# Rebuilding the second layer's dilated attention: products per token, norm factors in the weights, one maximum over the three groups, V held beside ones

## The chip, the cores and the metric

The kernel runs on one core of one Trainium2 chip. The metric is the device time of one execution in microseconds (us), the median of several runs. An instruction runs on TensorE (PE, its weight loads are PEld), VectorE (DVE), ScalarE (ACT) or GpSimd (POOL); SyncE (SP) issues most of the transfers.

## The reference, cut to what matters

One inference step of a two-layer decoder trunk on 512 new prompt tokens and 8 decode tokens (520 rows of 1024, float32). Layer 0 is stick-breaking attention and a mixture of experts. Layer 1, which the change touches, is attention over three dilated windows, and a second mixture of experts:

```python
kv = (rmsnorm(x, g_kv) @ w_kv).reshape(b, t, N_DIL, 2, N_KV_B, HEAD_DIM)     # 3 groups, 4 K/V heads of 64
k = rope(rmsnorm(kv[:, :, :, 0], k_norm), pos)                               # v = kv[:, :, :, 1]
q = rope(rmsnorm(rmsnorm(x, g_attn) @ w_q, q_norm), pos)                     # 3 groups, 16 query heads of 64
# group g attends over a window with dilation 1, 4, 16: o[g], lse[g]
# (the first over the block before and its own, the others here within the tokens of one residue)
w = softmax(stack(lses), axis=0)                                             # over the three groups
x = x + einsum('gbth,gbthe->bthe', w, stack(outs)).reshape(...) @ w_o
```

The normed and rotated K, and V, are outputs too. `rmsnorm(x, g)` is `x * rsqrt(mean(x*x) + eps) * g`.

## The kernel before

The stages follow one another, each in a block that ends with all engines meeting: layer 0's attention, its mixture of experts (`moe`), `layer_b`, then `moe` again. `moe` leaves two weighted rows per token in DRAM (`y_rows`). Its last block (L1347 to L1395) reads them back and adds them to the residual `x` (L1391), token tile by token tile; for layer 0 ACT squares each tile (L203) and POOL forms the factor `rs` (L211, L212).

`layer_b` (L1398) works on units: a unit is one K/V head j (0 to 3) in one group g, with 64 columns of V, 64 of K and 4 x 64 of the query heads that share them, 384 in all (`UW`), for all 520 tokens. `WINDOW` sets the order of groups in a head: 1, 2, 0. First `turn_normed` (L221) multiplies `x` by `rs` and by each of two gain rows (L252), turns the results so that the 1024 channels lie on partitions (L264) and copies them out (L242): `xkT` and `xqT`. The unit weights are fetched while this goes on (`load_unit`, L1416, queued by SP), and after that whenever a unit's products are done.

In the attention block PE follows an order written out by hand (`weave`, L1570):

- `project` (L1528): 128 of the 384 columns are the stationary operand, 260 tokens move. Six such chunks of 8 products each make a unit, and their results have tokens along the row: ACT copies them (L1689) and PE turns them back to tokens on partitions (`turn_tok`, L1547, L1555 and L1560), DVE copies these to `tok` (L1781).
- POOL then norms and rotates K and Q of the unit (`front`, L1899 to L1925). Only after this are K and Q turned again (`turn_back`, L1578), 12 transposes of 128x128 in a unit, and copied by ACT (L1709). The kernel runs two units ahead: the parts of `project` and `turn_tok` for unit n+2 are woven between the steps of unit n (`ahead`).
- For each of the 4 query heads in turn: `qk` (L1585), the scores in PSUM, four products of 64 rows x 128 columns (group 0: two of 128 and three of 256); `soft` on DVE (L1806 scales and masks, L1809 takes the maximum of each row, L1810 negates it); `exps` on ACT (L1715), which also sums; `turn_p` (L1604), `p_copy` on ACT (L1723), `pv` (L1613) with the turned probabilities as the stationary operand and V moving, 64 columns, and `o_copy` on DVE (L1814).
- Groups 1 and 2 have their tokens ordered by residue (t mod 4), so their outputs go to DRAM and back (`reorder`, L1492) to be put in order.
- `combine` on DVE (L1832) weighs the three groups by their maxima and sums; `turn_o` on PE (L1664) turns the result, DVE copies it to `oT` (L1869).

One pass of this loop over j takes three units. The next block has the output projection (L317, L326) and the decode tokens' attention.

Of the kernel before, what the change touches and what calls it, by code (L numbers as in the profile page):

```python
# [43 lines left out]
for _name, _width in (("ident", 128), ("tri", 128), ("strict", 128), ("ones", 128),  # L44
                      ("cos", NT * 8), ("sin", NT * 8), ("valid", NT), ("iota", NE), ("iota99", NE),
                      ("iota64", CAP), ("gid", 2 * NT), ("sid", 2 * NT), ("m0", 4 * 256), ("m1", 128), ("m2", 128), ("m3", 128), ("pidx", 1), ("sel8", DEC), ("eps", 1), ("eps64", NT), ("mhalf", NT)):
    CONST[_name] = (_at, _at + _width)
    _at += _width
# [4 lines left out]
def constants():  # L53
# [19 lines left out]
    put("sin", np.sin(ang))  # L73
    put("valid", np.stack([np.arange(128) < rows for _, rows in TILES], 1))
# [51 lines left out]
def flat(ap):  # L126
    return ap.rearrange("p a b -> p (a b)")

def build(nc, a, outs):  # L130
# [5 lines left out]
    o_rows = [nc.dram_tensor(f"o_rows{g}", [SEQ, 4 * 66], F32, kind="Internal").ap() for g in range(2)]  # L136
# [3 lines left out]
    with ExitStack() as ctx:  # L140
# [38 lines left out]
        ss, rs = sb("ss", [128, NT]), sb("rs", [128, NT])  # L179

# [633 lines left out]
        def moe(layer, norm, next_norm):  # L814
# [6 lines left out]
            wts = sb("wts" + L, [128, 2, NT], to=phM)  # L821
# [523 lines left out]
            last_norm[0] = norm  # L1345

            with ExitStack() as ph, nc.Block() as block:  # L1347
                yr = sb("yr" + L, [128, 2 * NT, D], to=ph)
                s_gt, s_cb = [lsem(f"y_back{k}") for k in range(2 * NT)], lsem("y_added")
                junk = sb("junk_c" + L, [128, D], to=ph)  # L1350
# [6 lines left out]
                @block.sync  # L1357
                def _(sp):
                    rows_back(sp, 0)
                    if next_norm:  # L1360
                        next_norm.load(sp)
                    else:
                        for t, rows in TILES:
                            sp.wait_ge(s_cb, 2 * t + 2)
                            dst = y_prompt[0, 128 * t:128 * t + 128, :] if t < 4 else y_sample[:, 0, :]
                            sp.dma_start(dst, x[0:rows, t, :]).then_inc(s_out, 16)
                        sp.wait_ge(s_out, 16 * NT)

                @block.scalar
                def _(act):  # L1370
                    rows_back(act, 1)
                    if next_norm:
                        for t in range(NT):
                            act.wait_ge(s_cb, 2 * t + 2)
                            next_norm.square(act, t, junk)

                @block.gpsimd
                def _(pool):
                    if next_norm:
                        pool_do.on(pool)  # L1380
                        for t in range(NT):
                            next_norm.power(pool, t)
                        pool_do.done()
# [14 lines left out]
        def layer_b(norm, next_norm):  # L1398

            phX = ExitStack()  # L1400
            UW = HD + KQ
            wB = sb("wB", [128, NDIL, KT, UW], to=phB)
            xkT = sb("xkT_b", [128, KT, TOK], to=phX)
            xqT = sb("xqT_b", [128, KT, TOK], to=phX)
# [4 lines left out]
            WINDOW = (1, 2, 0)  # L1409
            s_w = [sem(f"wb{g}_in") for g in range(NDIL)]  # L1410

            def kv_cols(j, g, part):

                return ds(g * 512 + part * 256 + j * HD, HD)

            def load_unit(sp, j, g):  # L1416
                sp.dma_start(wB[:, g, :, 0:HD], w_kv[:, :, kv_cols(j, g, 1)]).then_inc(s_w[g], 16)
                sp.dma_start(wB[:, g, :, HD:2 * HD], w_kv[:, :, kv_cols(j, g, 0)]).then_inc(s_w[g], 16)
                sp.dma_start(wB[:, g, :, 2 * HD:], w_q[:, :, ds(g * D + j * 256, 256)]).then_inc(s_w[g], 16)

            def first_units(sp):
                for g in WINDOW:
                    load_unit(sp, 0, g)

            norm.turn([xkT, xqT], prefetch=first_units)

# [3 lines left out]
            with phX, ExitStack() as ph, nc.Block() as block:  # L1430
                pT = sb("pT", [128, 3, TOK], to=ph)
                tok = sb("tok", [128, NDIL, NT, UW], to=ph)
                kk = sb("kk", [128, 4, 2 * HD], to=ph)
                kT = sb("kT", [128, SEQ], to=ph)
                qT = sb("qT", [128, 2, SEQ], to=ph)
                vp = sb("vp", [128, 2, 4, HD], to=ph)
                sc = sb("sc", [128, 2, 4, 256], to=ph)
                pTs = sb("pTs", [128, 2, 8 * 128], to=ph)
                nm = sb("nm", [128, 2, 4], to=ph)
                junk = sb("junk_b", [128, 1], to=ph)  # L1440
                ost = sb("ost", [128, NDIL, 4, 4, HD + 2], to=ph)
                cw = sb("cw", [128, 5, 4, 4], to=ph)
                ce = sb("ce", [128, NDIL, 4, 4], to=ph)
                oc = sb("oc", [128, 4, 4, HD], to=ph)
                ot = gain_row[:, :].rearrange("p (t h e) -> p t h e", t=4, h=4)
# [4 lines left out]
                s_kvo = [sem(f"b_kv_stored{g}") for g in range(NDIL)]  # L1450
                (s_gn, s_gain, s_proj, s_pev, s_tt, s_tk, s_vc, s_rope, s_tb, s_tbc, s_qk, s_sev, s_mx, s_ex, s_tp,
                 s_ptc, s_pv, s_oc, s_od, s_ob, s_cm, s_ce, s_comb, s_to, s_toc, s_kk) = (
                    sem("b_" + n) for n in (
# [655 lines left out]
```

## Time and profile before

| | us |
|---|---|
| median of 3 runs (1758.04 to 1768.62) | 1766.94 |
| the profiled execution, its own time | 1769.61 |
| its span, first to last instruction | 1767.8 |
| y rows asked for by SP, end of layer 0's experts | 747.07 |
| first projection of `layer_b` | 785.60 |
| last instruction of its attention block ends | 1337.08 |

### The profile page before, as it was taken

The page shows a single profiled execution, that of the slowest core. Times are in us where ns is not written, and L with a number is a line of the kernel's source. Part 1 is how long each engine was busy: PE and PEld are TensorE (multiplying, and loading weights), DVE is VectorE, ACT ScalarE, POOL GpSimd, SP SyncE. Part 2 cuts the span into 40 slices and gives each one's busy share as a digit, 9 for nine tenths or more (in the row PEclk, how much of TensorE's full clock was granted, in tenths as well). Part 3 has the DMA queues.
Part 4 walks back from the last instruction along what each step waited for, and adds up shares of the span by engine and source line. Part 5 has one row for each costly group of instructions (what it writes and reads, how often), then busy time and mean ns, then how long its engine had stood idle before and what let it go on. Part 6 is the DMA issues. An engine that isn't in the chain of part 4 may idle for free. (4 is left out here: it accounts for less than half of the span.)

```text
span 1767.8 us, 21720 instructions
## 1 busy us (share of the span) xinstructions
PE 1478.4 (84%) x8250; PEld 1069.6 (61%) x8250; DVE 606.3 (34%) x917; ACT 448.8 (25%) x959; POOL 485.3 (27%) x522
## 2 busy tenths in 40 slices
PE   5899999697699988559998998998885986999882
PEld 4677777443666554347887877887772444666451
DVE  1354443311411111161335436346335723111113
ACT  2233443311122211131333332433430111222110
POOL 3343334300011110015664564455400000111100
PEclk9999999899599999869999999999756966999997
DMA  7834323400989999462221221210305237999994
GB/s 265 290 103 135 104 72 108 168 1 0 350 318 421 420 421 420 201 206 58 75 75 43 67 63 42 66 33 0 126 27 154 94 119 300 412 420 421 421 409 169
DMA packets 148834, 335.72 MB, mean 190 GB/s; under 512 B 51832, under 2 KB 101464, under 8 KB 124064
## 3 DMA queue, kind: packets, MB, share of 16 engines
q1 hardware_dynamic: 133760, 296.73, 45.0%
q0 software_dynamic: 13824, 33.84, 5.3%
q10 hardware_dynamic: 1184, 4.26, 0.6%
q8 instruction: 43, 0.70, 0.2%
q14 instruction: 23, 0.19, 0.0%
HBM read 312.74 MB, written 38.55 MB: 199 GB/s over the span
## 5 line engine op out<-in xcount | busy, mean ns | idle before, releaser
L917 PE MATMUL ps<-wg,oT 128*64 128x256 f32 x1024 | 237.1, 385 | 19.3 <-DMA wd<-in_w_down 17.8
L917 PE MATMUL ps<-wu,oT 128*64 128x256 f32 x1024 | 237.3, 386 | 0.0
L917 PEld LDWEIGHTS ps<-wg,oT 128*64 128x64 f32 x1024 | 139.7, 139 | 75.7 <-DMA wd<-in_w_down 28.2
L1543 PE MATMUL ps<-xqT_b,wB 128*128 128x260 f32 x768 | 185.0, 397 | 0.0
L455 PE MATMUL ps<-xnT_a,wA 128*128 128x260 f32 (+1 forms) x768 | 172.7, 385 | 2.5 <-DMA wA<-in_w_qkv_a 1.3
L1543 PEld LDWEIGHTS ps<-xqT_b,wB 128*128 128x128 f32 x768 | 148.4, 197 | 24.2 <-issue 1.0
L455 PEld LDWEIGHTS ps<-xnT_a,wA 128*128 128x128 f32 x768 | 145.8, 192 | 27.0 <-issue 4.1
L917 PEld LDWEIGHTS ps<-wu,oT 128*64 128x64 f32 x1024 | 139.6, 139 | 36.3 <-issue 16.4
L1308 POOL DMA_INDIRECT y_rows<-ysb,idx x32 | 32.1, 1002 | 435.5 <-DVE ysb L952 435.5
L935 PE MATMUL ps<-wd,hT 128*64 128x512 f32 x512 | 124.0, 601 | 30.4 <-DVE hT L946 30.4
L778 POOL TENSOR_TENSOR work<-work,cst 128x128 f32<-128x128 f32 x128 | 74.5, 582 | 184.8 <-DVE work L703 147.5
L1806 DVE SCALAR_TENSOR_TENSOR sc<-ps,cst 128x512 f32<-128x512 f32 (+1 forms) x48 | 41.6, 867 | 194.5 <-PE ps L1600 112.5
L943 DVE TENSOR_TENSOR h<-sg,ps 64x256 f32<-64x256 f32 x64 | 26.4, 413 | 237.5 <-ACT sg L940 231.1
L1715 ACT ACTIVATE sc<-sc,nm 128x128 f32<-128x128 f32 (+1 forms) x192 | 81.3, 425 | 77.6 <-DVE nm L1810 77.6
L1905 POOL TENSOR_TENSOR sq<-tok 128x1600 f32<-128x1600 f32 x12 | 34.2, 2852 | 230.2 <-DVE tok L1781 230.2
L1543 PE MATMUL ps<-xkT_b,wB 128*128 128x260 f32 x384 | 94.6, 404 | 1.1 <-PEq L156 1.0
L508 PE MATMUL ps<-work,cst 128*128 128x128 f32 (+3 forms) x288 | 68.2, 399 | 31.0 <-POOL work L790 31.0
L952 DVE COPY ysb<-ps 64x512 f32<-64x512 f32 x64 | 44.4, 694 | 137.1 <-PE ps L935 137.1
L317 PE MATMUL ps<-wB,oT 128*128 128x512 f32 (+1 forms) x160 | 77.5, 649 | 12.0 <-DVE x L326 10.1
L1543 PEld LDWEIGHTS ps<-xkT_b,wB 128*128 128x128 f32 x384 | 75.9, 202 | 13.3 <-issue 1.3
L508 PEld LDWEIGHTS ps<-work,cst 128*128 128x128 f32 x288 | 49.3, 215 | 51.3 <-POOL work L790 34.3
L935 PEld LDWEIGHTS ps<-wd,hT 128*64 128x64 f32 x512 | 36.6, 136 | 70.2 <-issue 70.2
(263 smaller groups left out, 2336.6 us busy)
## 6 DMA issues: line engine op xcount, KB each, us to landing
wg<-in_w_gate SPq DMA_DIRECT2D x64, 1024.0 KB
wu<-in_w_up SPq DMA_DIRECT2D x64, 1024.0 KB
wd<-in_w_down SPq DMA_DIRECT2D x64, 1024.0 KB
wA<-in_w_qkv_a SPq DMA_DIRECT2D x24, 512.0 KB, 4.3
wB<-in_w_q_b SPq DMA_DIRECT2D x12, 1024.0 KB
wB<-in_w_kv_b SPq DMA_DIRECT2D x24, 256.0 KB
o_rows<-ost SPq DMA_DIRECT2D x8, 528.0 KB, 5.3
ost<-o_rows SPq DMA_DIRECT2D x8, 528.0 KB
```

The costliest lines, as they stand in the source:

```text
L317: last = nc.tensor.matmul(bank(6 + n)[0:rows, :], oT[:, m, 128 * t:128 * t + rows], self.w[m][:, 512 * n:512 * n + 512], start=(m == 0), s ...
L455: last = nc.tensor.matmul(bank(6 + h)[:, 0:half], wA[:, m, k, :], xnT[:, k, half * h:half * h + half], start=(k == 0), stop=(k == KT - 1))
L508: return nc.tensor.matmul(ps[:, b + o:b + o + width], lhs, rhs, start=start, stop=stop, skip_group_check=True)
L778: last = nc.gpsimd.tensor_tensor(v, v, mask, op)
L917: last = nc.tensor.matmul(bank(q)[lo:lo + CAP, 0:FE], x[:, k, :], wt[:, k, :], start=(k == 0), stop=(k == KT - 1))
L935: last = nc.tensor.matmul(bank(4 + q)[CAP * n:CAP * n + CAP, :], hT[:, q, f, :], wd[s][:, f, 512 * n:512 * n + 512], start=(f == 0), stop= ...
L952: return nc.vector.tensor_copy(ysb[w][CAP * q:CAP * q + CAP, 512:D], bank(4 + q)[CAP:2 * CAP, :])
L1308: pool.indirect_dma_start(out=y_rows, out_offset=rows_of(idx, 1, v), in_=ysb[v % 2][:, :], in_offset=None, bounds_check=2 * TOK - 1, oob_i ...
L1543: last = nc.tensor.matmul(bank(h)[:, 0:HALF], wB[:, g, kt, 128 * f:128 * f + 128], xT[:, kt, HALF * h:HALF * h + HALF], start=(kt == 0), s ...
L1715: last = nc.scalar.activation(sc[:, h % 2, b, 0:width], sc[:, h % 2, b, 0:width], ACT.Exp, bias=nm[:, h % 2, b:b + 1], accum_out=ost[:, g, ...
L1806: V.scalar_tensor_tensor(out=dst, in0=src, scalar=SCALE, in1=mask, op0=ALU.mult, op1=ALU.add).then_inc(s_sev, 1)
L1905: pool_do(P.tensor_tensor(sq[:, :, :], kq, kq, ALU.mult))
```

## The change

Only `layer_b` and what leads into it change; `moe` for layer 1 is as before.

- The adding of the experts' rows moves into the attention block. `x` is turned as it is, unnormed (`turn_x`), and there is one turned copy, `xT`.
- The gains `g_kv` and `g_attn` lie on partitions (`gcol`), and DVE multiplies each unit's weights by them, in place, before its first product (`scale`, two instructions, 8x128 and 8x256 elements a partition). The factor `rs` of a token is applied when its products are copied from PSUM. Groups 1 and 2 use it in residue order (`rsr`, which goes through DRAM once).
- `project`: 128 tokens of `xT` are the stationary operand, 384 weight columns move; for groups 1 and 2 the tokens are picked by residue, with tables `cosr`, `sinr` for the rotation. Four chunks of 8 products, one chunk of 8 products for the last 32 tokens in four column groups (32 columns wide each), and one product with `sel8` that sums these four. DVE copies each chunk from PSUM (`evict`) straight to `tok` and to `vo`, which holds V (64 columns) beside ones (64 columns). The ACT copies of projections, `turn_tok`, the turned V copy, the doubling copy into `kk` (now into `tok`) and their waits are gone. Three units are projected ahead instead of two, and the groups come in the order 0, 1, 2.
- Scores come in 8 steps in a pass (4, 2, 2) rather than 12, each for two heads, whose products alternate between partitions 0 to 63 and 64 to 127 and between two banks; `soft` takes 1024 elements in each step and keeps all scores of the pass in SBUF.
- One maximum per token and head: `far_max` and `near_max` join the groups' maxima; since they are in two orders, they cross through DRAM (`m_rows`, 16-byte pieces). The exponentials (`exps`, without a sum) start only after it, so after all scores of the pass.
- The probabilities are turned in 8 parts (`PARTS`; far = groups 1 and 2 of a head, near = group 0), half of each copied by ACT and half by DVE (`p_copy`). `weigh`: `vo` is the stationary operand and the turned probabilities move, 128 columns. The output is turned already, with its sum in partitions 64 to 127. `finish_head` on DVE copies the far half in token order, adds the near half, takes the reciprocal of 64x512 sums and multiplies into `oT`. `combine`, `turn_o`, `reorder` and `o_copy` go.

The diff, cut to what the prediction speaks of:

```diff
+                    def turn_x(t, rows):
+                        pe.wait_ge(s_cb, 2 * t + 2)
...
+                            for kt in range(KT):
+                                last = nc.tensor.matmul(bank(c % 2)[:, 0:UW], xT[:, kt, cols], wB[:, g, kt, :],
+                                                        start=(kt == 0), stop=(kt == KT - 1))
...
+                    def scores(j, g, s):
...
+                            return nc.tensor.matmul(bank(4 + h)[:, o:o + width], qT[r, pair, 128 * b:128 * b + 128],
+                                                    kT[r, 128 * kb:128 * kb + width], start=True, stop=True)
...
+                        if g:
+                            for b in range(4):
+                                for h in range(2):
+                                    last = product(h, b, b, 128 * b, 128)
...
+                                for g in (1, 2):
+                                    o = 512 * (g - 1) + 128 * b
+                                    last = nc.tensor.matmul(out, vo[:, j % 2, g, b, :], P[:, o:o + 128],
+                                                            start=(g == 1), stop=(g == 2))
...
+                        turn_back(j, 0, 0)
+                        turn_back(j, 0, 1)
+                        ahead(0, 0)
+                        turn_back(j, 0, 2)
+                        ahead(0, 1)
+                        scores(j, 0, 0)
+                        ahead(0, 2)
+                        scores(j, 0, 1)
+                        ahead(0, 3)
+                        scores(j, 0, 2)
+                        ahead(0, 4)
+                        scores(j, 0, 3)
+                        ahead(0, 5)
...
+                        turn_back(j, 2, 0)
+                        turn_back(j, 2, 1)
+                        ahead(1, 4)
+                        turn_back(j, 2, 2)
+                        ahead(1, 5)
+                        scores(j, 2, 0)
+                        ahead(2, 0)
+                        scores(j, 2, 1)
+                        ahead(2, 1)
+
+                        turn_p(j, 0)
+                        ahead(2, 2)
+                        turn_p(j, 1)
+                        weigh(j, 0)
+                        ahead(2, 3)
...
+                        turn_p(j, 3)
+                        weigh(j, 2)
+                        ahead(2, 5)
+                        for i in range(4, NPART):
+                            turn_p(j, i)
+                            weigh(j, i - 1)
+                        weigh(j, NPART - 1)
...
+                    def scale(j, g):
+                        dve.wait_ge(s_w[g], 48 * j + 48)
+                        for i, (lo, hi) in enumerate(((0, 2 * HD), (2 * HD, UW))):
+                            w = wB[:, g, :, lo:hi]
+                            V.tensor_tensor(w, w, gcol[:, i].unsqueeze(2).to_broadcast([128, KT, hi - lo]), ALU.mult).then_inc(s_ws, 1)
...
+                            V.tensor_scalar(tok[:, g, c, HD:], bank(c % 2)[:, HD:UW], r, None, ALU.mult)
+                            V.tensor_scalar(vo[:, j % 2, g, c, 0:HD], bank(c % 2)[:, 0:HD], r, None, ALU.mult).then_inc(s_ev, 1)
+                        elif c == 4:
+                            V.tensor_copy(part[:, :], bank(0)[:, 0:UW]).then_inc(s_ev, 1)
...
+                    def finish_head(j, h):
+                        dve.wait_ge(s_pv, NPART * j + PARTS.index((h, 1)) + 1)
+                        b = 2 + 2 * (h % 2)
+                        dve_do(V.tensor_copy(osum.rearrange("p (i r) -> p r i", r=4), bank(b).rearrange("p (r i) -> p r i", r=4)))
+                        V.tensor_tensor(osum, osum, bank(b + 1), ALU.add).then_inc(s_oc, 1)
+                        dve.wait_ge(s_oc, 4 * j + h + 1)
+                        dve_do(V.reciprocal(orec[0:HD, :], osum[HD:2 * HD, :]))
+                        dve_do(V.tensor_tensor(oT[64 * (h % 2):64 * (h % 2) + 64, 2 * j + h // 2, 0:SEQ], osum[0:HD, :], orec[0:HD, :], ALU.mult))
...
+                        soft(j, 0, 2)
+                        if more:
+                            scale(j + 1, 1)
+                        ahead(0, 4)
+                        soft(j, 0, 3, s_m0)
+                        ahead(0, 5)
...
+                        ahead(1, 3)
+                        if more:
+                            scale(j + 1, 2)
+                        ahead(1, 4)
+                        ahead(1, 5)
...
+                        p_copy(j, 3)
+                        finish_head(j, 0)
+                        ahead(2, 5)
+                        p_copy(j, 4)
+                        finish_head(j, 1)
+                        if j < NKV - 2:
+                            scale(j + 2, 0)
+                        p_copy(j, 5)
+                        p_copy(j, 6)
+                        finish_head(j, 2)
+                        p_copy(j, 7)
+                        finish_head(j, 3)
```

In the last part, which is DVE's, `ahead` is `evict` of the next pass's unit. Before its product c, `project` waits for the eviction of product c-2 of the same bank, and product 5 for that of product 4. `turn_p(i)` waits for the exponentials of part i and both copies of part i-1, `weigh(i)` for both copies of part i.

## Rows read from the trace of the kernel before

**Rows 1.** Table by stage: window, length, busy PE PEld DVE ACT POOL, clock, DMA share, GB/s
```profile
747.00:785.60 38.60, 13.34 (x80) 11.97 (x81) 25.36 (x20) 14.39 (x20) 8.03 (x10) 0.62 0.81 248
...
1104.30:1230.60 126.30, 119.02 (x678) 101.05 (x677) 56.85 (x86) 43.50 (x139) 66.56 (x52) 0.96 0.12 35
1230.60:1337.10 106.50, 82.23 (x379) 70.44 (x376) 45.30 (x74) 35.95 (x121) 28.05 (x24) 0.63 0.17 64
```

**Rows 2.** Timeline of PE in a pass: start, us, line, operands, records, [idle before]
```profile
1154.13 1.16 PE L1600 MATMUL ps<-kT,qT 64*128 64x128 f32 x8
1155.21 0.66 PE L1610 MATMUL ps<-cst,sc 128*128 128x128 f32 x4
1155.71 1.00 PE L1624 MATMUL ps<-vp,pTs 128*128 128x64 f32 x8
1156.55 3.73 PE L1543 MATMUL ps<-xqT_b,wB 128*128 128x260 f32 x16
...
1173.87 0.71 PE L1597 MATMUL ps<-kT,qT 64*128 64x128 f32 x4
1174.42 1.46 PE L1593 MATMUL ps<-kT,qT 64*128 64x256 f32 x6
1175.81 3.77 PE L1543 MATMUL ps<-xqT_b,wB 128*128 128x260 f32 x16
1179.51 0.71 PE L1597 MATMUL ps<-kT,qT 64*128 64x128 f32 x4
...
1219.42 0.66 PE L1582 MATMUL ps<-cst,kk 128*128 128x128 f32 x4 [2.88 <-ACT qT L1709]
1219.92 5.36 PE L1543 MATMUL ps<-xkT_b,wB 128*128 128x260 f32 x16
```

**Rows 3.** Timeline of PE in layer 0: products that share or change rows of the array
```profile
98.18 2.43 PE L494 MATMUL ps<-qkvT 64*128 64x512 f32 x16
100.54 14.19 PE L455 MATMUL ps<-xnT_a,wA 128*128 128x256 f32 x64
...
312.47 3.65 PE L508 MATMUL ps<-work,cst 128*128 128x512 f32 x18
315.95 7.18 PE L455 MATMUL ps<-xnT_a,wA 128*128 128x260 f32 x32
```

**Rows 4.** Timelines of DVE at 1178 and of POOL then
```profile
1178.43 2.58 DVE L1810 TENSOR_SCALAR nm<-ost 128x4 f32<-128x4 f32 x1
...
1178.07 2.91 POOL L1915 TENSOR_TENSOR tok<-tok,sq 128x1600 f32<-128x1600 f32 x1
```

**Rows 5.** Single lines: durations in ns (min/median/max), first and last start, forms
```profile
L1862 DVE TENSOR_TENSOR oc<-oc,gain_row x8: 1225/1226/3824, 969.4 to 1332.6; 128x1024 f32<-128x1024 f32 x8
...
L1781 DVE COPY tok<-ps x60: 534/548/559, 809.6 to 1258.5; 128x384 f32<-128x384 f32 x48, 8x384 f32<-8x384 f32 x12
...
L326 DVE TENSOR_TENSOR x<-x,ps x18: 675/689/689, 376.9 to 1436.3; 128x512 f32<-128x512 f32 x16, 8x512 f32<-8x512 f32 x2
...
L1810 DVE TENSOR_SCALAR nm<-ost x48: 169/172/3357, 849.9 to 1313.3; 128x4 f32<-128x4 f32 x48
...
L1715 ACT ACTIVATE sc<-sc,nm x192: 384/390/510, 850.1 to 1315.1; 128x128 f32<-128x128 f32 x128, 128x256 f32<-128x256 f32 x64
```

**Rows 6.** Single lines: two of the reciprocals, of 5 and of 16 elements
```profile
L1223 DVE RECIPROCAL wts<-st x2: 191/191/191, 484.6 to 1482.7; 128x5 f32<-128x5 f32 x2
...
L1855 DVE RECIPROCAL cw<-cw x4: 253/253/253, 965.9 to 1326.6; 128x16 f32<-128x16 f32 x4
```

**Rows 7.** Timeline of DVE from the experts' end to the first projection
```profile
751.93 7.89 DVE L1391 SCALAR_TENSOR_TENSOR x<-yr,wts,x 128x1024 f32<-128x1024 f32 x6 [12.36 <-DMA yr<-y_rows]
760.34 5.22 DVE L1391 SCALAR_TENSOR_TENSOR x<-yr,wts,x 128x1024 f32<-128x1024 f32 x4 [0.52 <-DMA yr<-y_rows]
```

**Rows 8.** Timeline at the end of the attention block: weighing, last copy
```profile
1303.99 3.09 PE L1621 MATMUL ps<-tok,pTs 128*128 128x64 f32 x14
...
1335.85 1.23 DVE L1869 COPY oT<-ps 128x1024 f32<-128x1024 f32 x1 [2.06 <-PE ps L1669]
```

More of the change, by code:

```diff
@@ L73, in constants @@
     put("sin", np.sin(ang))
+    by_residue = np.stack([4 * np.arange(128) + r for r in range(4)] + [np.full(128, PAST)], 1).astype(np.float32)
+    ang = (by_residue[:, :, None] * inv[None, None, :].astype(np.float32)).astype(np.float32)
+    put("cosr", np.cos(ang))
+    put("sinr", np.sin(ang))
     put("valid", np.stack([np.arange(128) < rows for _, rows in TILES], 1))
@@ L813, in moe @@
         @scoped
-        def moe(layer, norm, next_norm):
+        def moe(layer, norm):
             L = str(layer)
@@ new lines, in turn_p @@
+                    def turn_p(j, i):
+                        h, near = PARTS[i]
+                        q = NPART * j + i
+                        pe.wait_ge(s_ex, q + 1)
+                        for n in range(2):
+                            pe.wait_ge((s_pta, s_ptd)[n], q)
+                            if near:
+                                blocks = [(0, b, 2 * (b - 2 * n) + half, half) for b in (2 * n, 2 * n + 1) for half in range(2) if b or half]
+                            else:
+                                blocks = [(1 + n, r, r, 0) for r in range(4)]
+                            for g, b, o, half in blocks:
+                                last = nc.tensor.transpose(bank(6 + n)[:, 128 * o:128 * o + 128],
+                                                           sc[g][:, h, b, 128 * half:128 * half + 128], ident)
+                            last.then_inc(s_tp, 1)
@@ L1747, in _ @@
[L1747 to L1758 removed]
+                    rows_back(act, 1)
@@ new lines, in exps @@
+                    def exps(j, i):
+                        h, near = PARTS[i]
+                        act.wait_ge(s_nn if near else s_nr, j + 1)
+                        if near:
+                            for b in range(4):
+                                v = sc[0][:, h, b, (0 if b else 128):256]
+                                last = nc.scalar.activation(v, v, ACT.Exp, bias=neg[:, 1, b, h:h + 1])
+                        else:
+                            for g in (1, 2):
+                                for r in range(4):
+                                    v = sc[g][:, h, r, :]
+                                    last = nc.scalar.activation(v, v, ACT.Exp, bias=neg[:, 0, r, h:h + 1])
+                        last.then_inc(s_ex, 1)
@@ L1925, in front @@
                         P.tensor_tensor(x2, rp[:, 2], rp[:, 3], ALU.add).then_inc(s_rope, 1)
[L1927 to L1932 removed]
+                    for j in range(NKV):
+                        for g in range(NDIL):
+                            front(j, g)
+                    pool_do.done()
+            last_norm[0] = norm
             n1, n2 = PAST // 4 + 1, PAST // 16 + 1
```

763 lines of the change are left out of this document (346 added, 417 removed).

## The prediction

> **What bounds the kernel now.** Only layer B's attention changes, so I read from it outwards. The table by stage [rows 1] gives one pass of the loop over j, 126.3 us, in which PE is busy for 119.0, DVE for 56.9, ACT for 43.5, POOL for 66.6: PE's instruction stream is the bound. The stage before, 38.6 us, has PE busy for only 13.3; the last stage, from 1230.6 to the end of the block, has it busy for 82 of 106.5 us at a mean clock of 0.63. So the rebuilt stage gains from fewer PE instructions as long as nothing stops PE, it can gain before the first projection, and it can lose where DVE, which gets more work, becomes late. What a product takes I read from starts in PE's timeline [rows 2]; a stop of 2.88 us also stands there.
>
> **Before the first projection.** It starts at 785.60 (the table of times). The experts' rows arrive as before and the ten additions end at 760.34 + 5.22 = 765.6 [rows 7]. What followed (norm, turning two copies, two blocks' ends) goes: `turn_x` follows each tile's addition, and DVE goes on to `scale(0, 0)`. That is two instructions with 1024 and 2048 elements; 1024 elements take 1.23 us in the nearest row, L1862 [rows 5], so 3.7 us with gaps. The weights of the first unit are queued behind the rows, which come in the same 13 us; I count no wait. For one more meeting of engines ahead of the block I take 1.3 us (an estimate; 0 to 4). First projection at 770.6, 15.0 us earlier.
>
> **PE's work in a pass.** The old pass less its idle time (7.3) and less what the lower clock cost (mean 0.96 of 126.3 us, 5.0) is 114.0 us [rows 1].
> - Projection and turning. A chunk of 8 products with 260 columns takes 3.70 us (1175.81 to 1179.51) [rows 2], 0.463 a product, 0.03 over its columns at 2.4 GHz with four passes. A unit has six, 22.2, plus 15 to 19 transposes at 0.12 (four in 0.50, L1610), 2.3 on average. New: 32 products of 384 columns at 0.64 + 0.03 = 21.4, the fifth chunk in two rounds of four side by side 1.3, `sel8` 0.65: 23.4. Three units save 3.3.
> - Scores. Old: 32 products of 128 columns at 0.27 (1154.13 to 1155.21 is four), and four heads of group 0 at 0.55 + 1.39 [rows 2]: 16.4. New: pairs on different rows of the array. Layer 0's L494 does such pairs: two heads of 1280 columns each, which would take 4.27 us one after the other, take 2.36 [rows 3]. For a pair of 128 columns the ends are 0.22 (full overlap) and 0.54 (none). Four products with 64 columns (L1624) take 0.84 although their columns are 0.43, so loading the stationary operand sets 0.21 a product; two loads one after the other are 0.42, and I take 0.40. For 256 columns, 0.46. 20 and 6 pairs: 10.8. Saved 5.6 (2 to 9).
> - Turning the probabilities: four transposes fewer, 0.5. `turn_o`: 1.0.
> - Weighing. Old: 60 products at 0.21 [rows 2], 12.6. New: 60 products of 128 columns, for which L1600 gives 0.27 and L508's mix (nine products, 2048 columns in 3.48 us) 0.22 [rows 2, 3]. I take 0.265, near the row of the same size: 15.9, 3.3 more.
>
> This leaves 106.9 us of PE in a pass, 7.1 less. All of it would show if PE never waited longer than before.
>
> **What stops PE in a pass.** DVE works in order, so I lay its instructions beside PE's.
> - `ahead(0, 5)` waits for the copy of product 4, which stands behind `soft(0, 2)` (2.5 us: 1024 elements twice, each as L1862), `scale` (3.7) and 0.55 (L1781) [rows 5]; PE has 2.3 us of work meanwhile: 4.8 lost. `ahead(1, 5)` likewise, with 2.9 us of work against 5.3: 2.4. Small waits 0.8.
> - `turn_p(0)` needs the last `soft` (2.5), the joined maximum (0.6 and waits for POOL, 2) and 8 exponentials. These were 0.39 each (L1715, 128 elements; 0.51 with 256) and had a sum beside them; the ends are 0.13 (the difference of the two, if all else overlaps) and 0.39, I take 0.3. 7.5 to 8.2 us against the 5.3 of `ahead(2, 1)`: 2.9.
> - The tail. `finish_head` is a copy and an addition from PSUM at 0.69 (L326), a reciprocal, and a product at 0.69 [rows 5]. A reciprocal of 5 elements takes 191 ns, of 16 elements 253 ns [rows 6]: 5.6 ns an element. No row has 512; a linear run gives 253 + 496 x 5.6 = 3.05 us, and the ends are 0.69 (a copy's rate) and 8.1 (if nothing of the 253 ns were fixed). I take 3.1, since every DVE row of few elements has such a fixed part (L1810: 4 elements in 0.17 [rows 5]), so 5.2 us a head. From the end of `weigh(2)` to the copy before `weigh(7)` DVE has three heads 15.6, `scale` 3.7, four copies 2.8, a part 0.6, a wait for `weigh(5)` 1.4, and waits for POOL: an instruction with operands in SBUF waits for POOL's, as L1810, 0.17 of work in 2.58 us until L1915 ended [rows 4]; L1862 once took 3.82 [rows 5]. Four such of about 1 us. Together 28.1. PE has 12.6 of work there: 15.5 lost, in the third pass, which has no `scale` there, 11.8.
> - Clock: the old pass had the lower clock after stops of 3 us (16 records then took 5.36 instead of 3.7 [rows 2]); two more of 1.7 us: 3.4.
>
> A pass is 106.9 + 10.9 + 15.5 + 3.4 = 136.7 us, the third 133.0, against 126.3. What the removed stalls had cost (7.3) is in the subtraction above.
>
> The reciprocal is where the Trainium skill speaks against this change more than the rows do: "VectorE: DVE Perf Modes", section "First, the fixed hardware budget", says that it runs as an iterative divide with a repeat count of 8. At that page's 0.96 GHz, eight cycles are 8.3 ns an element, 4.4 us for 512 (an estimate by that page). By it ten heads would cost 1.3 each more than I count, 13 in all: 1791. The rows' slope is lower.
>
> For the scores, "TensorE: Matmul & The Clock Gate", section "The mechanism", says that weight loads overlap running matmuls only where their row groups differ; by it pairs would overlap fully and a pass would gain 4 us more. No row here has pairs of 128 columns alone, and the sum does not use this.
>
> **First units and last pass.** Three units ahead: 3 x (23.4 + 0.8) = 72.6, and 3 for the clock, which starts low (0.62 before the stage [rows 1]): 75.6. In the last pass nothing is projected. The clock was low when this happened before [rows 1, 8]: seven products of 64 columns took 3.1 us, 0.44 each instead of 0.21. So PE's pieces double: eight steps of scores at some 2.1 us, each with 1.5 in which DVE reads them (29), and three rounds of turning and copying K and Q at 3.3 make 39 us, then 6 for maximum and exponentials, eight parts of turning and weighing at 5.8 are 46 (DVE's 2 x 0.7 + 5.2 for two parts hides in them), last head 5.2: 96 us. At the full clock it would be 74. The last instruction of the block was at 1335.85 + 1.23 = 1337.1 [rows 8].
>
> Covers: POOL's work, 66.6 us a pass [rows 1], is the same and fits. DVE's evictions, 0.75 a chunk, hide under the next chunk's 5.4; the copies that leave ACT cost nothing there and save nothing. The maxima's way through DRAM is hidden by `ahead(2, 1)` to `ahead(2, 3)`, except in the last pass, where it could cost 3. While SP waits for it, the stores of later groups and the weights of the pass after next stand behind, needed 40 us later or more.
>
> **Sum.** 770.6 + 75.6 + 136.7 + 136.7 + 133.0 + 96 = 1348.6, 11.5 us later than 1337.1. The rest of the kernel is the same. The profiled execution, 1769.6, becomes 1781.1; the median stands 2.7 below it: 1778.
>
> **The rivals.**
> - DVE is not late (not slower). If the reciprocal goes at a copy's rate, a head costs 2.8 instead of 5.2, three passes lose 7.5 us less and the end 2.4: 25 us less, 1753. Place: the tail of a pass. It decides below 2 us a reciprocal. Against it: the slope [rows 6].
> - The clock stays at 2.4 GHz. `weigh` moves 128 columns through all 128 rows and columns where `pv` moved 64. Then the last pass is 74, the start loses 3 less and the passes 10: 35 less, 1743. Against it: the last stage's 0.63 with PE busy for 77% [rows 1].
> - The tail takes the clock down. PE works for 12.6 of 28 us there; at half the rate these are 25, and the work after it starts slow: 5 a pass, 15 in all, 1793.
> - The reciprocal is longer than its slope: at 5.6 us, halfway to the upper end, each head takes 2.5 more, three heads in each of three tails and one at the end, 25 us, and in the last pass DVE is then the slower one for 5 more: 1808. Against it: the slope again.
>
> **How the numbers follow.** Forecast 0.37 (own range 1763 to 1793), not late 0.16, full clock 0.16, low clock in the tails 0.20, long reciprocal 0.11. 1% is 17.7 us, about what can be told from no change: 1749 to 1785. Faster takes the full clock and its meeting with the first rival, 0.22; slower takes the last two and the upper third of the forecast, 0.40; the same 0.38. With the unknowns of scores (+6, -10 over three passes) and weighing (-9) the range is 1743 to 1808.
>
> **What would show it.** A pass of 130 to 140 us; stops of PE before `weigh(7)` and `turn_p(6)` put down to DVE's copy; a reciprocal near 3 us; chunks of 5.3 us; a first projection near 771; a clock near 0.5 in the last pass. I am wrong if DVE is idle in the tail, or if the pass is at 115.

## The result, and the profile after

The changed kernel takes 1753.95 us in the median of 20 runs, the kernel before 1766.18 in as many: a ratio of 0.9938 (0.9920 to 0.9955), faster by 0.6%. (One run of each kernel was far slower, 2096.62 and 4430.95 us; the ratio leaves them out.) I had forecast 1778, slower by 0.6%. The profiled execution took 1750.27 us (before 1769.61); my sum for it was 1781.1, so it is 30.8 too high. Where these lie the table by stage of the changed kernel shows (columns as in [rows 1]): the time to the first projection, the three units ahead of the passes, three full passes, the last pass, the rest.

```profile
747.00:767.10 20.10, 8.94 (x41) 7.24 (x41) 16.78 (x14) 9.42 (x15) 8.09 (x8) 0.50 1.10 328
767.10:840.70 73.60, 71.56 (x246) 54.01 (x246) 22.68 (x37) 0.42 (x1) 45.73 (x35) 0.97 0.28 72
840.70:976.70 136.00, 114.41 (x568) 90.71 (x568) 68.15 (x78) 26.85 (x69) 92.75 (x71) 0.91 0.20 52
976.70:1113.10 136.40, 114.14 (x567) 91.15 (x566) 73.05 (x81) 25.68 (x68) 69.46 (x51) 0.91 0.16 40
1113.10:1240.10 127.00, 111.56 (x568) 88.78 (x567) 67.71 (x79) 25.69 (x68) 62.74 (x45) 0.94 0.12 39
1240.10:1320.30 80.20, 47.62 (x321) 40.89 (x320) 54.81 (x49) 25.33 (x67) 4.09 (x7) 0.76 0.04 8
1320.30:1748.50 428.20, 335.47 (x1938) 200.86 (x1938) 132.71 (x230) 62.39 (x116) 36.18 (x43) 0.88 0.77 301
```

The same cuts through the kernel before, made afterwards: two units ahead, the passes together, the last pass [rows 1] and the rest.

```profile
785.60:838.80 53.20, 50.18 (x231) 41.41 (x231) 7.65 (x14) 6.56 (x14) 21.99 (x17) 0.97 0.21 56
838.80:1230.60 391.80, 366.82 (x2087) 310.96 (x2087) 176.03 (x261) 135.71 (x424) 219.44 (x164) 0.97 0.19 53
...
1337.10:1767.80 430.70, 338.14 (x1938) 202.23 (x1938) 132.71 (x230) 62.39 (x116) 36.15 (x43) 0.87 0.77 299
```

The difference, 19.3 us, is read off these: the first projection starts 18.5 earlier. From there to the block's end the new attention takes 553.2 us and the old took 551.5: units ahead +20.4, three passes +7.6, last pass -26.3. The rest is 2.5 shorter. So the gain is nearly all made ahead of the attention: the new attention as a whole gave nothing, and its three full passes are longer, although PE's busy time in them fell from 366.8 to 340.1.

Why, PE's timeline of the first pass shows: three stops in its tail, each put down to DVE's copy of turned weights (`arena_b` is the tile that holds them), besides two before `sel8` products.

```profile
873.05 0.81 PE L1554 MATMUL ps<-part,cst 128*8 128x384 f32 x2 [4.02 <-DVE part L1801]
...
906.81 0.81 PE L1554 MATMUL ps<-part,cst 128*8 128x384 f32 x2 [1.82 <-DVE part L1801]
...
922.50 1.09 PE L1616 MATMUL ps<-cst,arena_b 128*128 128x128 f32 x8 [0.21 <-ACT arena_b L1739]
...
950.50 1.11 PE L1616 MATMUL ps<-cst,arena_b 128*128 128x128 f32 x4 [3.58 <-DVE arena_b L1851]
...
960.97 1.11 PE L1616 MATMUL ps<-cst,arena_b 128*128 128x128 f32 x4 [5.09 <-DVE arena_b L1851]
...
973.56 3.33 PE L1637 MATMUL ps<-arena_b,vo 128*128 128x128 f32 x14 [5.42 <-DVE arena_b L1851]
```

DVE's timeline at the last two of the three shows what stands before the copies: a whole head finish each (copy, addition, reciprocal, product), and before the first of them the weight scale too.

```profile
950.38 1.07 DVE L1857 COPY gain_row<-ps 128x512 f32<-128x512 f32 x1
951.48 0.69 DVE L1858 TENSOR_TENSOR gain_row<-gain_row,ps 128x512 f32<-128x512 f32 x1
952.20 3.35 DVE L1860 RECIPROCAL gain_row<-gain_row 64x512 f32<-64x512 f32 x1
955.58 0.79 DVE L1861 TENSOR_TENSOR oT<-gain_row 64x512 f32<-64x512 f32 x1
956.40 3.91 DVE L1780 TENSOR_TENSOR wB<-wB,gcol 128x1024 f32<-128x1024 f32 x2
960.24 0.68 DVE L1851 COPY arena_b<-ps 128x512 f32<-128x512 f32 x1
...
965.11 1.09 DVE L1857 COPY gain_row<-ps 128x512 f32<-128x512 f32 x1 [2.29 <-PE ps L1637]
966.24 0.69 DVE L1858 TENSOR_TENSOR gain_row<-gain_row,ps 128x512 f32<-128x512 f32 x1
966.96 3.35 DVE L1860 RECIPROCAL gain_row<-gain_row 64x512 f32<-64x512 f32 x1
970.34 2.34 DVE L1861 TENSOR_TENSOR oT<-gain_row 64x512 f32<-64x512 f32 x1
972.72 0.69 DVE L1851 COPY arena_b<-ps 128x512 f32<-128x512 f32 x1
```

The last pass has such stops in its second half as well. PE's timeline there:

```profile
1277.17 1.97 PE L1616 MATMUL ps<-cst,arena_b 128*128 128x128 f32 x8 [5.76 <-ACT arena_b L1739]
...
1296.16 0.66 PE L1616 MATMUL ps<-cst,arena_b 128*128 128x128 f32 x4 [3.98 <-DVE arena_b L1851]
...
1302.71 0.66 PE L1616 MATMUL ps<-cst,arena_b 128*128 128x128 f32 x4 [2.03 <-DVE arena_b L1851]
...
1312.56 1.80 PE L1637 MATMUL ps<-arena_b,vo 128*128 128x128 f32 x14 [3.43 <-DVE arena_b L1851]
```

### The profile page after: what moved, and what is told of

Read it like the earlier page. It is cut to its first block and busy times, and to the rows that moved or that the text cites. A ratio compares the mean times of both kernels' runs of the same rounds, so it can differ in the third digit from the quotient of the medians.

```text
span 1748.5 us, 19682 instructions
## 1 busy us (share of the span) xinstructions
PE 1429.7 (82%) x7782; PEld 1006.5 (58%) x7782; DVE 657.1 (38%) x888; ACT 369.6 (21%) x668; POOL 490.8 (28%) x522
## 5 line engine op out<-in xcount | busy, mean ns | idle before, releaser
L1544 PE MATMUL ps<-wB,xT_b 128*128 128x384 f32 x768 | 264.6, 501 | 6.5 <-DVE vo L1799 3.6
L1544 PEld LDWEIGHTS ps<-wB,xT_b 128*128 128x128 f32 x768 | 205.6, 273 | 52.0 <-issue 6.4
L948 DVE TENSOR_TENSOR h<-sg,ps 64x256 f32<-64x256 f32 x64 | 26.4, 413 | 236.9 <-ACT sg L945 236.9
L217 POOL TENSOR_TENSOR ss<-ss,cst 128x1 f32<-128x1 f32 (+1 forms) x20 | 5.4, 269 | 278.4 <-ACT junk_s L209 171.9
L1616 PE MATMUL ps<-cst,arena_b 128*128 128x128 f32 x240 | 41.5, 320 | 36.4 <-DVE arena_b L1851 29.1
L954 ACT ACTIVATE ysb<-ps 64x512 f32<-64x512 f32 x64 | 37.7, 589 | 152.5 <-PE ps L940 152.5
L945 ACT ACTIVATE sg<-ps 64x256 f32<-64x256 f32 x64 | 24.3, 380 | 210.6 <-PE ps L922 210.6
## 6 DMA issues: line engine op xcount, KB each, us to landing
wg<-in_w_gate SPq DMA_DIRECT2D x64, 1024.0 KB, 16.8
```

Of the source, the lines that this page charges most:

```text
L954: return nc.scalar.activation(ysb[w][CAP * q:CAP * q + CAP, 0:512], bank(4 + q)[0:CAP, :], ACT.Copy)
L1544: last = nc.tensor.matmul(bank(c % 2)[:, 0:UW], xT[:, kt, cols], wB[:, g, kt, :], start=(kt == 0), stop=(kt == KT - 1))
L1616: last = nc.tensor.transpose(bank(6 + n)[:, 128 * o:128 * o + 128], sc[g][:, h, b, 128 * half:128 * half + 128], ident)
```

## The experiments

The theory after this reading: the passes are held by VectorE's order (finishes, scales, copies), not by its load, and the last pass came out shorter than forecast because its wider products kept TensorE at 2.4 GHz for half of it. Rivals: the reciprocal fills idle time only; the pairs of scores made the difference; the clock goes by something else. Ends of the block are read at the first product of the output projection, 1320.82 in the changed kernel and 1337.40 in the one before; the last pass is then 80.7 us long.

**The reciprocal as a copy.**

```diff
-dve_do(V.reciprocal(orec[0:HD, :], osum[HD:2 * HD, :]))
+dve_do(V.tensor_copy(orec[0:HD, :], osum[HD:2 * HD, :]))
```

> The changed kernel with the reciprocal of the denominators replaced by a copy of them; the division is so left out (each head's sum is multiplied by its denominator). It is read by the end of the attention block, 1320.3 us in the changed kernel, not by the total, because other numbers go into the router behind it. Theory (DVE's late copies of turned weights, held behind the reciprocal of 3.35 us, are what stops TensorE in the tail of every pass): of the 14.1 us of stops in the tail of a pass some 9 go, of the 9.4 in the last pass some 7, and the last reciprocal's 3 at its end: the block ends 35 us earlier, at about 1285. Rival (the tail is held by the weight scale and by GpSimd's port, and the reciprocal only fills idle time): the block ends less than 10 us earlier.

The kernel leaves out the division, and it is a single run, read by its trace. The output projection began at 1297.88, 22.9 us earlier: two thirds of what the theory said, over twice the rival's bound. The passes became 1.7, 1.7, 8.0 and 11.4 us shorter. In the first pass the stop of 3.58 became 0.65, but the others became 7.17 and 6.71. DVE's timeline there:

```profile
946.18 0.42 DVE L1860 COPY gain_row<-gain_row 64x512 f32<-64x512 f32 x1
946.64 0.68 DVE L1861 TENSOR_TENSOR oT<-gain_row 64x512 f32<-64x512 f32 x1
...
953.48 4.54 DVE L1780 TENSOR_TENSOR wB<-wB,gcol 128x1024 f32<-128x1024 f32 x2
...
964.47 2.50 DVE L1860 COPY gain_row<-gain_row 64x512 f32<-64x512 f32 x1
967.01 3.92 DVE L1861 TENSOR_TENSOR oT<-gain_row 64x512 f32<-64x512 f32 x1
```

The same copy takes 0.42 and 2.50 us, the same product 0.68 and 3.92, while GpSimd's timeline has it at work on `tok` and `sq` from 948 to 970 without a break (2.92 and 3.62 us for two instructions at 963.8 and 966.8). So it looks as if waits for GpSimd took most of what the reciprocal gave up in the first two passes; this is read from what ran at the same time, and no run moved GpSimd's work. The first rival of the prediction had 25 us for a shorter reciprocal, 7.5 in each full pass and 2.4 at the end: the sum is near 22.9, the places are not, and half of it lay in the last pass, where I had hidden VectorE's finishes under PE's work.

**The heads' scores one after the other.** In `scores`, for all three forms of its products:

```diff
-for b in range(4):
-    for h in range(2):
+for h in range(2):
+    for b in range(4):
         last = product(h, b, b, 128 * b, 128)
```

> The changed kernel with the score products of head 0 issued first and then those of head 1, instead of one of each in turn. Theory (two products of 64 rows on different halves of the array run side by side, 0.27 us a pair of 128 columns): a pair costs 0.5 us or more, the scores of a pass 16 us of TensorE instead of 8.6, and the three full passes become 7 us longer each; in the last pass half of it hides in waits: block end about 1345. Rival (what makes the scores cheap is only their number of columns, not the order): pairs stay under 0.30 us and the block ends at 1320 within 3 us.

```profile
888.65 1.71 PE L1585 MATMUL ps<-kT,qT 64*128 64x128 f32 x16
```

In the next such step the following instruction starts 1.64 us later, 0.41 for two products of 128 columns; in the changed kernel the row of the same 16 records has 1.16 us and its next instruction starts 1.09 later, 0.27 a pair. For 256 columns nothing changed (1.14 against 1.13 for eight records). So the order is worth 2.8 us a pass (four times 0.55, twice 0.32), not 7. The block ended far later all the same, at 1351.96: the first pass took 136.7 us (before this edit 135.9), the second 149.2 (136.5), the third 135.7 (127.0), the last 88.9 (80.7). Of the second's 12.8 us one new stop of 5.09, for the exponentials, and a clock of 0.87 instead of 0.91 are seen; in the last pass the clock is 0.69 instead of 0.76. That any of this follows from the order of the scores is not shown, and it is a single run. Both readings fell in part: the order matters, and less than I said.

**The last pass's weighing in products of 64 columns.**

```diff
-for b in range(4):
-    out = bank(...)[:, 128 * b:128 * b + 128]
+W = 64 if j == NKV - 1 else 128
+for b, c in [(b, c) for b in range(4) for c in range(0, 128, W)]:
+    out = bank(...)[:, 128 * b + c:128 * b + c + W]
```

> The changed kernel with each weighing product of the last pass cut into two of 64 columns, as wide as the kernel before had them; nothing is left out. It is read in the second half of the last pass (from 1280 to the first product of the output projection, 1320.8 in the changed kernel, mean granted clock 0.83 there). Theory (the weighing's 128 columns a product are what gives the last pass back half of the clock): the clock there falls to 0.6 or less, and the output projection begins 5 us later or more. Rival (the clock goes by how TensorE's work and stops follow each other, not by the products' width): the clock stays at 0.75 or more and the start moves by less than 3 us.

The last pass took 104.2 us instead of 80.7, in a single run. Table by stage of this kernel, from its start of the last pass:

```profile
1247.70:1280.00 32.30, 19.01 (x142) 13.94 (x140) 24.64 (x20) 5.76 (x11) 0.00 (x0) 0.76 0.08 18
1280.00:1321.00 41.00, 34.96 (x190) 34.36 (x191) 13.99 (x18) 18.52 (x54) 0.00 (x0) 0.59 0.01 1
1321.00:1352.00 31.00, 22.58 (x113) 22.18 (x112) 16.18 (x13) 1.09 (x2) 0.00 (x0) 0.54 0.00 1
```

and of the changed kernel in the middle window:

```profile
1280.00:1321.00 41.00, 25.01 (x173) 24.13 (x174) 28.15 (x25) 14.13 (x39) 0.00 (x0) 0.83 0.00 1
```

PE was busier, 85% against 61%, and had the lower clock, 0.59 against 0.83. So a stage that is busier can have the lower clock. What of the edit does it is not told apart: it halves the width, doubles the number of weight loads, and changes where PE stops. Nor are the 24 us the price of the clock alone: at 2.4 GHz 16 products of 64 columns take 3.52 us (row below, next start at 1321.78), 0.22 each, as long as one of 128, so the edit doubles the weighing's work too.

```profile
1318.26 3.68 PE L1643 MATMUL ps<-arena_b,vo 128*128 128x64 f32 x32
```

**Filler in the last weaves of the kernel before, and in the last pass of the one after.** Where the projections are missing:

```diff
+pe.wait_ge(s_tk, 5 * NDIL * NKV)
+pe.wait_ge(s_vc, NDIL * NKV)
+nc.tensor.matmul(bank(0), xkT[:, 0, 0:128], xkT[:, 1, 0:512], start=True, stop=True)
```

> The kernel before, with products that nobody reads (128 x 128 by 512 columns, 0.87 us each at 2.4 GHz) at the places of the missing projections in the last two of its weaves, 18 of them. Theory (before, TensorE ran at 1.2 GHz from 1275 to 1353 because nothing streamed wide in its waits, and its work there was the bound): the granted clock of the last two weaves rises to 0.9 or more, and the attention block ends 10 to 18 us earlier than 1337.1 in spite of 16 us of added work. Rival (the clock stays or another engine bounds these weaves): it ends 10 to 16 us later.

> The changed kernel with the same kind of product at the 18 places of the missing projections in its last pass, and one behind each of the last four weighing steps. Theory (the last pass is held by VectorE in its second half and by TensorE's clock only in its first): the mean clock of the last pass rises from 0.76 to over 0.9, and the block ends 0 to 6 us earlier than 1320.3. Rival (the added work lies on the path): it ends 8 us or more later.

Kernel before with filler, from 1258 to the projection's start:

```profile
1258.00:1290.00 32.00, 29.33 (x152) 20.14 (x150) 13.83 (x23) 12.98 (x44) 21.98 (x17) 0.89 0.49 185
1290.00:1327.00 37.00, 23.23 (x138) 17.33 (x136) 21.17 (x36) 12.52 (x37) 0.00 (x0) 0.86 0.05 15
```

Without it the same stretch is 32 us at 0.60 and 47 us at 0.50 (in cuts of one us the clock was low from 1264 to 1343, not from 1275 to 1353 as I had put down). The trace has 32 records of the added products: 16, not 18. With them the projection began at 1327.74 instead of 1337.40, and the whole took 1757.74 us, 0.9959 (0.9931 to 0.9986) of before. So the clock did cost the old last weaves their length, by a little less than expected. In the changed kernel, with 22 such products, the mean clock rose too (0.88 and 0.92 in the two halves), but the projection began at 1322.86, 2.0 later, and the last pass had begun 1.9 later: no gain and no loss, where the theory had up to 6 us and the rival 8 the other way. The last pass then waits for VectorE: DVE's copies end PE's stops of 2.24, 2.80 and 2.55 us in its tail. What a higher clock would be worth there without the added work, no run shows.

**VectorE's order.** Four kernels, each built on the last or beside it. ScalarE copies the second half of the turned weights in steps 4 to 7:

```diff
 nc.scalar.activation(pT[:, q % 2, lo:512], bank(6)[:, lo:512], ACT.Copy).then_inc(s_pta, 1)
+if i >= 4:
+    act.wait_ge(s_tp, 2 * q + 2)
+    nc.scalar.activation(pT[:, q % 2, 512:1024], bank(7), ACT.Copy).then_inc(s_ptd, 1)
```

> The changed kernel with the second half of the turned weights of steps 4 to 7 of each pass copied out of PSUM by ScalarE behind its own half, instead of by VectorE behind the head finishes; nothing is left out. Theory (only VectorE's order stops the tail): the stops of 3.58, 5.09 and 5.42 us shrink to under 2 us each, 10 us less in each of three passes and 8 in the last: 1750 becomes about 1713. Rival (the stop moves to the wait for the head's sum being read out of its banks, with the weight scale of 3.9 us between two finishes): less than half of it, 1735 or more.

Measured: 1713.64 us (0.9707 of before, 0.9661 to 0.9753). The stops in the tails went, as the theory had it; 3.8 us came back at the head of the next pass, behind the scale. The total was hit, its parts were not: in the traces the three full passes are 19.3, 11.3 and 8.5 us shorter where I had 10 each, and PE's busy time in the first fell by 7 with the stops, at a clock of 0.97 instead of 0.91; the last pass is 81.9 us, nothing less where I had 8. VectorE's finishes then came behind PE instead of between its products: 6.80 us of stop ahead of the last pass's first scores, and 12.74 at its end instead of 6.47.

The scales moved, with a third argument that picks one of the two instructions (conditions on `j` are left out here):

```diff
 soft(j, 0, 0)
+scale(j + 1, 1, (0,))
 ahead(0, 2)
 soft(j, 0, 1)
+scale(j + 1, 1, (1,))
...
 soft(j, 0, 2)
-scale(j + 1, 1)
...
+scale(j + 1, 2)
 ahead(1, 0)
 ahead(1, 1)
 soft(j, 1, 0)
+scale(j + 2, 0, (0,))
 ahead(1, 2)
 soft(j, 1, 1)
+scale(j + 2, 0, (1,))
 ahead(1, 3)
-scale(j + 1, 2)
...
 finish_head(j, 1)
-scale(j + 2, 0)
```

> The changed kernel with VectorE's weight scales split in two and moved to places where it waits: between the first scores of a pass, before the second group's copies, and out of the tail; nothing is left out. Theory (a scale in VectorE's order costs TensorE its length where a copy is due behind it): the stops of 4.02 and 1.82 us in the middle of a pass go (5 us in each of three passes) and 4 us of the tail's in the two passes that had a scale there: 23 us less, about 1727. Rival (the scale is hidden and the stops have other causes): within 6 us of 1750.

Measured: 1732.25 us (0.9822, 0.9775 to 0.9870; four runs from 1723.67 to 1736.27): 22 less. The stops before `sel8` are 0.68 in it.

> Both edits at once: the turned weights' second half copied by ScalarE in steps 4 to 7, and VectorE's weight scales split and moved to where it waits. Theory (each removes its own stops, and with the copies on ScalarE the scale in the tail had become a stop of 3.8 us at the head of the next pass): 1713.6 less 5.8 in three passes less 3.8 in two: about 1689. Rival (they remove the same stops): 1708 or more.

Measured: 1688.73 us (0.9569, 0.9543 to 0.9595). The edits remove different stops. Of what was left VectorE's timeline in the first pass shows this (first copy of the second group's tokens, and the joined maximum):

```profile
886.17 0.55 DVE L1802 TENSOR_SCALAR tok<-ps,rsr 128x320 f32<-128x320 f32 x1 [9.80 <-DMA q_rows<-tok]
...
916.80 0.17 DVE L1840 TENSOR_TENSOR neg<-mres,mo 128x16 f32<-128x16 f32 x1
```

and SyncE's queue before it:

```profile
872.54 0.39 SPq L1477 DMA_DIRECT2D m_rows<-mx  x1
...
880.98 0.46 SPq L1472 DMA_DIRECT2D q_rows<-tok  x1
```

The first copy of a group waits for the store of the same buffer, and the store stands in SyncE's queue behind the wait for a maximum. Moved ahead:

```diff
-store_kv(j, 0)
+for g in range(NDIL):
+    store_kv(j, g)
 near_max(j)
 next_weights(j + 2, 0)
-store_kv(j, 1)
 next_weights(j + 2, 1)
-store_kv(j, 2)
 far_max(j)
```

> The kernel with both edits (1688.7 us), and on SyncE's queue the stores of all three groups of a pass ahead of the maxima and of the next weights. Theory (VectorE's first copy of the second and of the third group's tokens waits for these stores, which stand behind a wait for the last score maximum and for a projection; TensorE stops 2.4 to 2.9 us at one and, through the exponentials, 2.0 and 1.8 us at the other): some 11 us less in three passes, about 1678. Rival (the stores land late anyway, or push the weights' loads back): within 3 us of 1688.7 or slower.

Measured: 1679.54 us (0.9503, 0.9480 to 0.9527), 9.2 less.

The copy of each head's first sum on ScalarE, on top of the two edits (it reads PSUM in order and writes with a stride of four elements):

```diff
-dve_do(V.tensor_copy(osum.rearrange("p (i r) -> p r i", r=4), bank(b).rearrange("p (r i) -> p r i", r=4)))
+osum, orec = sums[h % 2]
+dve.wait_ge(s_oa, 4 * j + h + 1)
...
+nc.scalar.activation(sums[h % 2][0].rearrange("p (i r) -> p r i", r=4),
+                     bank(2 + 2 * (h % 2)).rearrange("p (r i) -> p r i", r=4), ACT.Copy).then_inc(s_oa, 1)
```

> The kernel with both edits, and the strided copy of each head's first sum (1.08 us on VectorE) on ScalarE too, with a second pair of buffers. Theory (in the last pass VectorE's four head finishes of 5.9 us in a row set the end of the block, 12.7 us behind TensorE's last product, and 6.8 us of stop ahead of the last pass's first scores): 4 us off at each of the two places, 8 us less than with both edits, about 1681. Rival (ScalarE's copy of the odd-strided bank comes as late as VectorE's did): the same time as with both edits within 2 us.

Measured: 1683.93 us (0.9516, 0.9481 to 0.9552): 4.8 less than with both edits, between theory and rival, and not clear of the noise: its four runs go from 1674.53 to 1690.67, and the traced one is the slowest. The last stop fell from 12.75 to 7.02 and the one ahead of the last scores from 6.78 to 0.85; but in each full pass a `turn_p` now waits 1.25 for ScalarE, and one instruction of 16 elements a partition met GpSimd's work, as VectorE's timeline of this kernel shows:

```profile
917.90 2.83 DVE L1852 TENSOR_TENSOR neg<-mres,mo 128x16 f32<-128x16 f32 x1
```

2.83 us instead of the 0.17 of the same instruction above; GpSimd's instruction on `tok` ran from 917.79 to 920.70. The exponentials, and PE with them, came 3.8 later. So the last kernel has ScalarE's reads in the last two passes only, the stores first, and in the last pass:

```diff
 def ahead(g, c):
     if j < NKV - 1:
         project(j + 1, g, c)
+    elif g < 2 or c < 2:
+        fill()
```

> The kernel with both edits and the stores first, and in the last two passes the strided copy of each head's first sum on ScalarE (stops of 6.8 and 12.7 us), and in the score half of the last pass nine products that nobody reads, in TensorE's waits. Theory: 8 us less by ScalarE's copies and 2 by the clock, 10 us below the kernel with the stores first, about 1668. Rival (ScalarE's copies stand in the way of its copies of the turned weights, as they did in the first two passes, and the added products lie on the path): within 3 us of the kernel with the stores first.

Measured: 1672.35 us (0.9469, 0.9445 to 0.9494), 81.6 us below the changed kernel: 7.2 of the 10 expected on top of the stores. The edit adds 14 products (28 records in the trace), not nine. The share of ScalarE's reads and that of the filler were not taken apart. Its full passes are 105.1, 107.4 and 110.7 us. In the first of them PE hardly stops, and the clock is full:

```profile
844.35:949.48 105.13, 104.15 (x568) 83.08 (x567) 60.91 (x70) 28.62 (x73) 80.70 (x57) 1.00 0.27 70
```

## Why the prediction was wrong

The forecast was a slower kernel, 11.5 us later at the end of the attention block; it ended 16.8 earlier. The sum missed by 30.8 us: 3.5 ahead of the first projection, 2.0 in the units ahead, 7.0 in the three full passes, 15.8 in the last pass, 2.5 in the rest. Half of it, and enough to turn the sign, is one step.

- **Last pass, 96 forecast, 80.2 measured: the failed step.** I wrote that "PE's pieces double", and that VectorE's finishes hide in them. The scores and turning took 31.3 us (39 forecast), maximum and exponentials 5.8 (6), the eight parts of turning and weighing 37.2 (46), the last head 5.9 (5.2). The clock was low for about 38 of the 80 us only (mean 0.76), so the pieces did not all double; and in the second half VectorE, which I had hidden, stopped PE for 3.98, 2.03 and 3.43 us. That VectorE's finishes set the length there two runs speak for: with a copy for the reciprocal the pass was 11.4 us shorter, and with the clock up at 0.90 it was as long as before. I had the rival beside it (128 columns where 64 moved) at 0.16, and argued against it from the old stage's 0.63 with PE busy for 77%. That row could not speak against it: in the narrow weighing PE is 85% busy at 0.59. How the 15.8 us divide between the clock and the rest of the step is open.
- **Passes, 136.7, 136.7, 133.0 forecast, 135.9, 136.5, 127.0 measured.** The tail's stops were right (15.5 against 14.1), and that they are VectorE's order is shown by the copies on ScalarE. That the first two totals fit is luck, since the sizes inside cancelled. The same 568 records take 104.2 us of PE at full clock in the last kernel, where I had 106.9; the first pass had 114.4, so the clock after the stops cost 10.2, where I had 3.4; all stops together were 21.6, where I had 26.4. Scores were 0.27 a pair instead of 0.40, 2.2 less a pass. The Trainium skill, "TensorE: Matmul & The Clock Gate", section "The mechanism", lets weight loads overlap matmuls on other row groups. The trace agrees for 128 columns (0.27 in turn, 0.41 with the heads one after the other), while for 256 columns the order made no difference here. Weighing: 0.265 taken, 0.224 measured, 2.5 less; some 2 us more lie elsewhere in PE's work and were not found. The wait for the exponentials: 2.9 forecast, 0.2 measured, since the way from the last scores to them took 5.8 us, without the 2 for GpSimd.
- **The stores.** I had them "needed 40 us later or more". In the changed kernel too VectorE's first copy of the second group waits for a store, 13.29 us until 889.19, and PE stops for 1.45 behind it; on top of the two edits moving the stores ahead was worth 9.2 us. This term stood at nothing.
- **Reciprocal, 3.1 forecast, 3.35 measured** in all 16. The slope of two small rows [rows 6] carried to 512 elements within 8%. By the estimate from the Trainium skill, "VectorE: DVE Perf Modes", section "First, the fixed hardware budget", it would have been 4.4. The measurement decides against it. The copy out of PSUM that writes with a stride of four, 0.69 taken from L326, was 1.08.

```profile
L1860 DVE RECIPROCAL gain_row<-gain_row x16: 3347/3348/3350, 945.1 to 1316.2; 64x512 f32<-64x512 f32 x16
```
```profile
L1857 DVE COPY gain_row<-ps x16: 1054/1082/1100, 943.3 to 1314.4; 128x512 f32<-128x512 f32 x16
```

- **First projection, 770.6 forecast, 767.1 measured**: the additions ended at 763.1, 2.5 sooner than before, the 1.3 for a meeting of engines did not come, and a wait of 0.6 for weights did. Units ahead 75.6 against 73.6; the clock was up 4 us after they began. The rest, taken as the same, was 2.5 shorter: the clock rose 4 us into the output projection, where it had risen 5.5 us into it before, which explains about one of them.
- The rivals: full clock in the last pass, 74, is nearer than my 96, without its gain in the passes (0.91 there). The long reciprocal and the reciprocal at a copy's rate fell with 3.35. A lower clock in the tails was there: the clock cost a pass 6.8 more than the sum has for it, and the rival had 5 more. It did not show in the total because other terms were too large.

## What to carry to other kernels

An engine that is half busy can set the pace of one that is the bound: read what stands ahead of each late instruction in its order, and move long work (finishes, scales, stores) to where that engine waits, before counting what the bound engine saves. Here copies, scales and stores were worth 74.4 us, and 81.6 with the last kernel's two further edits, where the rebuilt attention by itself gave nothing. A stop costs more than its length where the clock is low after it: ten us a pass here. When a clock level is carried over from an old stage, ask whether the new one issues the same products. And when a total fits, lay its terms beside the trace: here two passes fit within a us with most of their terms off.

## What the hardware showed beyond what I expected

- TensorE at 85% busy with products of 64 columns had a mean granted clock of 0.59, at 61% busy with products of 128 columns 0.83, and in the kernel before 16 unread products of 512 columns went with a rise from 0.60 and 0.50 to 0.89 and 0.86.
- A VectorE instruction on 16 elements took 2.83 us while one of GpSimd's ran beside it (917.79 to 920.70), and 0.17 in another run; a copy of 64 x 512 took 0.42 and 2.50. With the reciprocal shortened, such long instructions stood in the first two passes' tails.
- Cutting the moving operand in two cost the whole again: a product of 64 columns took 0.22 us, one of 128 took 0.224, at 2.4 GHz.
